# Attention probabilities: weights brought in through a diagonal in the turning product

## The reference, cut to what matters

```
s_s = s_s - slopes[None, :, :, None, None, None] * d_s[:, :, None].astype(f32)
p_s = _masked_softmax(s_s, m_s)
o_s = jnp.einsum('bgrqm,bgqmd->bqgrd', p_s, v_sel)
...
p_w = _masked_softmax(s_w, m_w)
o_w = jnp.einsum('bgrqk,bkgd->bqgrd', p_w, vwb)

return (gb[:, :, 0, :, :, None] * o_c + gb[:, :, 1, :, :, None] * o_s
        + gb[:, :, 2, :, :, None] * o_w)
```

## Time and profile before

| | |
|---|---|
| three runs, median | 1534.01 us (1532.36 to 1534.39) |
| profiled execution | 1536.8 us, span 1535.0 us |
| PE busy | 1368.0 us, 89% of the span |
| DVE busy | 814.4 us, 53% |
| ACT busy | 438.7 us, 29% |
| POOL busy | 908.5 us, 59% |
| mean granted clock of TensorE | 0.956 |
| attention over tokens (first scores to the next stage's first product) | 1003.8 to 1183.4 us |

### The profile page before, as it was taken

One profiled execution on the slowest core, in us unless ns is written; L12 is line 12 of the kernel. 1 busy time (PEld: TensorE's weight loads), 2 busy tenths in 40 slices (PEclk: granted clock), 3 DMA queues, 4 the chain that ended last, 5 costly groups with the idle time before them and its releaser, 6 DMA issues.

```text
span 1535.0 us, 23038 instructions
## 1 busy us (share of the span) xinstructions
PE 1368.0 (89%) x8212; PEld 1059.6 (69%) x8212; DVE 814.4 (53%) x1386; ACT 438.7 (29%) x816; POOL 908.5 (59%) x704
## 2 busy tenths in 40 slices
PE   4979768797999899998959999988898979999986
PEld 2758668684887678887827878745555858878874
DVE  3754797414999921176032904368875136842312
ACT  3025620304321113300051112277765041331102
POOL 3859401073999988899627982900000837658962
PEclk9989978999999999999979999999999989999999
DMA  4213100023332443335717330300001519733321
GB/s 149 69 55 90 55 1 3 7 76 80 97 95 76 171 135 106 96 105 150 232 36 212 96 96 21 97 1 1 2 1 41 206 56 213 221 117 94 97 77 62
DMA packets 86048, 137.95 MB, mean 90 GB/s; under 512 B 16464, under 2 KB 34384, under 8 KB 84816
## 3 DMA queue, kind: packets, MB, share of 16 engines
q1 hardware_dynamic: 48384, 88.10, 19.5%
q10 hardware_dynamic: 37584, 48.71, 10.0%
HBM read 119.02 MB, written 20.91 MB: 91 GB/s over the span
## 4 chain that ended last, share of the span: by engine, by line
PE 74%; DVE 11%; issue 5%; POOL 5%; ACT 4%; DMA 1%; DVEq 0%; ACTq 0%; POOLq 0%
PE ps L353 18%; PE ps L355 18%; PE ps L354 18%; POOL wh L1178 4%; PE ps L346 3%; PE ps L661 3%; PE ps L673 2%; PE ps L650 2%; DVE xs L1245 2%; DVE uL L1235 1%; PE ps L494 1%; PE ps L731 1%; DVE bigB L1675 1%; PE ps L599 1%; DVE bigB L1355 1%
## 5 line engine op out<-in xcount | busy, mean ns | idle before, releaser
L1178 POOL TENSOR_TENSOR wh<-raw,small 128x512 fp32r<-128x512 f32 x336 | 413.4, 1230 | 347.6 <-PE ps L355 336.9
L1180 POOL TENSOR_TENSOR wl<-raw,wh 128x512 fp32r<-128x512 f32 x336 | 482.1, 1435 | 26.3
L353 PE MATMUL ps<-uH,wh 128*128 128x512 f32 x800 | 323.2, 404 | 33.8 <-DVE uL L1235 33.6
L354 PE MATMUL ps<-uL,wh 128*128 128x512 f32 x800 | 317.7, 397 | 0.0
L355 PE MATMUL ps<-uH,wl 128*128 128x512 f32 x800 | 317.3, 397 | 0.0
L353 PEld LDWEIGHTS ps<-uH,wh 128*128 128x128 f32 x800 | 153.7, 192 | 80.1 <-issue 27.7
L355 PEld LDWEIGHTS ps<-uH,wl 128*128 128x128 f32 x800 | 154.0, 193 | 33.0
L354 PEld LDWEIGHTS ps<-uL,wh 128*128 128x128 f32 x800 | 154.2, 193 | 31.0 <-issue 0.5
L353 PE MATMUL ps<-ffH,wh 128*128 128x512 f32 x256 | 102.7, 401 | 17.0 <-POOL wl L1180 16.8
L354 PE MATMUL ps<-ffL,wh 128*128 128x512 f32 x256 | 99.9, 390 | 0.0
L355 PE MATMUL ps<-ffH,wl 128*128 128x512 f32 x256 | 99.8, 390 | 0.0
(11 more groups left out here) (346 smaller groups left out, 2284.5 us busy)
## 6 DMA issues: line engine op xcount, KB each, us to landing
raw<-wstream SPq DMA_DIRECT2D x336, 256.0 KB, 2.6
b_powers_scratch<-bigB ACTq DMA_DIRECT2D x4, 1024.0 KB, 4.8
c_powers_scratch<-bigB ACTq DMA_DIRECT2D x8, 512.0 KB, 4.8
lags_scratch<-lag_rows_scratch ACTq DMA_DIRECT2D x8, 512.0 KB, 7.6
bigB<-b_powers_scratch ACTq DMA_DIRECT2D x4, 1024.0 KB, 8.2
bigB<-lags_scratch ACTq DMA_DIRECT2D x4, 1024.0 KB, 6.7
bigB<-c_powers_scratch ACTq DMA_DIRECT2D x4, 1024.0 KB, 9.5
hT<-x ACTq DMA_DIRECT2D x1, 2048.0 KB, 8.9
```

Source lines behind the costliest of these rows:

```text
L353: pe.matmul(out, lh, rh, start=first, stop=False)
L354: pe.matmul(out, lh, rl, start=False, stop=False)
L1178: pool.tensor_tensor(wh[:, j, :], raw[:, j, :], zero_ap.to_broadcast([128, 512]), ALU.add).then_inc(half_lead, 1)
L1180: pool.tensor_tensor(wl[:, j, :], raw[:, j, :], wh[:, j, :].bitcast(f32), ALU.subtract).then_inc(half_split, 1)
```

## The change

`turn` is no longer a transposing product with the unit matrix but an ordinary product, whose moving operand is a diagonal matrix with the rows' weights. `weigh` no longer touches the probabilities: it multiplies the unit matrix with the weights, for each of the two heads, into a new buffer `diag` (two buffers by u, two heads). It waits until the turn of unit u-2 has read the buffer of the same number.

```
+        diag = place("diag", [128, 2, 2, 128])
...
             def turn(u):
...
                 for half in range(2):
                     for kt in range(qt + 1):
-                        i = pe.transpose(ps[:, 4 + half, kt * 128:(kt + 1) * 128], prob[:, u % 3, half, kt * 128:(kt + 1) * 128], ident)
+                        i = pe.matmul(ps[:, 4 + half, kt * 128:(kt + 1) * 128], prob[:, u % 3, half, kt * 128:(kt + 1) * 128],
+                                      diag[:, u % 2, half, :], start=True, stop=True)
                 i.then_inc(at_t, 1)
...
             def weigh(u):
                 t, qt, b = UNITS[u]
-                W = (qt + 1) * 128
                 dve.wait_ge(at_e, u + 1)
                 own(dve.reciprocal(asum[:, u % 3, :], asum[:, u % 3, :]))
                 own(dve.tensor_tensor(asum[:, u % 3, :], asum[:, u % 3, :], gate[:, qt, 1 + b, t::KT], ALU.mult))
+                if u >= 2:
+                    dve.wait_ge(at_t, u - 1)
                 for half in range(2):
-                    i = dve.tensor_scalar(prob[:, u % 3, half, 0:W], prob[:, u % 3, half, 0:W], asum[:, u % 3, half:half + 1], None, ALU.mult)
+                    i = dve.tensor_scalar(diag[:, u % 2, half, :], ident, asum[:, u % 3, half:half + 1], None, ALU.mult)
                 i.then_inc(at_p, 1)
```

## The result

The changed kernel takes 1554.91 us (median of 4 runs, 1553.65 to 1558.17), the kernel before 1534.2 us in the same series (4 runs). The ratio is 1.014, with a 95% interval of 1.0121 to 1.0159: 20.7 us slower. The profiled execution of the changed kernel is the slowest of its runs, 1558.17 us with a span of 1556.4 us.

The account below looks back on a forecast made before the run. TensorE was taken as nearest to full in the attention stage, busy 18.7 of 21.2 us per head pair. Added passes +35.8, waits -15.3 and clock -3.9 made +16.6 us on 1534.01: forecast 1550.5 us, range 1543 to 1561.

Parts of the forecast that it names:

- the main term: TensorE in the attention stage: 320 turning products cost 0.112 us more each, +35.8 us.
- The second record: Each ordinary turning product leaves two TensorE records instead of one, 640 in all; +35.8 us.
- The gates: TensorE's three waits per head pair, before turns at 1059.43, 1065.95 and 1075.80: 1.96 of 2.51 us gained, 15.3 in all.
- late gates: TensorE's waits before turns of eight products; 1.60 us at 1065.95, with 0.35 taken as left.
- The clock: Two attention periods partly at half clock recover as the long wait mostly goes; -3.9 us.
- Rival 1: Attention stage: clock does not come back, or falls elsewhere; +20.5 us, 1554.5 us; chance 0.25.
- Rival 2: Attention waits stay because VectorE's chain follows a late TensorE; +35.8 less 0 to 5, 1565 to 1570 us; chance 0.08.
- rival 3: The turning product is carried out in one record, so nothing is added on TensorE; 1523 us; chance 0.04.
- rival 4: Loads of weights do not overlap between short turning groups; +88 us on TensorE, 1598 us; chance 0.02.
- The costs of nothing: In attention, VectorE's new wait for unit u-2's turn, the diagonals' buffer and ScalarE's work each add 0.

Follow-up runs that it names:

- e7: Kernel before, with two more 128 x 512 VectorE operations in one unit of each head pair, ahead of its late multiplication; 1545.25 us (one run).
- e8: Changed kernel, with four more 128 x 512 VectorE operations in one unit of each head pair, ahead of the late gate; 1591.08 us (one run).
- e3: Changed kernel without VectorE's new wait for the turn of unit u-2; 1554.94 us, ratio 1.0141.
- e5: Kernel before, but VectorE signals after each head's multiplication and TensorE waits for each head's before turning it; 1523.33 us, ratio 0.9933.
- e9: Kernel of e5, with GpSimd making the slopes only after VectorE's late multiplication of the same unit; 1518.03 us, ratio 0.9899.
- e4: Changed kernel with exponentials and diagonals written in fp32r, so the turning product is an ordinary fp32r one; 1564.39 us, ratio 1.0205.
- e2: Changed kernel's diagonals and new wait, but turning by transposing product with the unit matrix, weights missing from the output; 1518.8 us, ratio 0.9909 against the kernel before.
- e6: Kernel of e4 with each fp32r turning product issued twice to the same place; 1564.9 us (one run).

## Why the prediction was right

Forecast 1550.5 in 1543 to 1561, slower; measured 1554.9. The working held; the main term was too small by 4 us, and the clock's by 0.8.

- **The second record.** 640 records, 0.112 us apart: (1.98 - 0.64) / 12 = 0.112, just line 486's row. But I counted 0.112 us a product and nothing for the group. By the starts, two, four, six and eight products went from 0.36, 0.58, 0.80 and 1.02 us to 0.64, 1.09, 1.54 and 1.98 (before: rows 4 and the two lines of it above, where four products take 0.59 and in other head pairs 0.58; after: above). The differences, 0.28 + 0.51 + 0.74 + 0.96, twice in a period and eight times, are 39.8 us where the term had 35.8. The 4 us are 0.06 us for each of the 64 groups, and make the period 24.15 us where 23.7 to 23.9 were foretold. This is the term that was mis-sized most.
- **The gates.** 15.2 us gained, against 15.3. In a head pair: the first gone as said, the second 0.47 where I took 0.35 (range 0.12 to 0.53), the third gone where 0.2 was left. GpSimd disturbs the short form as well: 0.90 against 0.48 us for a pair (rows above), and without GpSimd the wait is gone. That the sums agree so closely is partly luck. I took all 19.7 us as waits at three gates in eight equal periods; 1.33 of them stand before the stage's first turn and stayed (1.32), and the last two late gates had only 0.86 and 1.28 us to lose. At the gates 3.2 us are left where I left 4.4.
- **The clock.** Behind the filling no stretch of the changed kernel's trace is at half clock. They cost more than the 3.9 us of the sum: the second, from 1131.21 to 1154.81, ends at a late gate where GpSimd does nothing and the wait is 0.86 and not 1.60 us (the line below, of the kernel before). At the full clock it would have been 21.23 - 0.74 = 20.49 us long, so it lost 3.1 us and not 2.37, and both together 4.7. The reason that I gave, the long wait, is supported by e7 and e8 (a longer wait, more half clock), though four of six equal waits before had none. The rule of the Trainium skill that I had left beside it ("TensorE: Matmul & The Clock Gate", Part 4) is not.

```profile
1154.81 1.09 PE L661 MATMUL ps<-const_table,bigB 128*128 128x128 f32 x8 [0.86 <-DVE bigB L1689]
```

- **The rest.** 39.8 - 15.2 - 4.7 = 19.9 us; the stage shows 19.6. The medians differ by 20.7, since they also hold what other stages do: the profiled execution of the changed kernel reached the stage 1.2 us later (1004.98 against 1003.77) and took 0.6 us longer behind it. The clock's term is read from one execution of each kernel. The mean clock of the kernel before goes from 0.954 to 0.966 over its executions, and the profiled one has 0.956; so that the median execution loses 4.7 us too is not shown.
- **The rivals.** Rival 1 named 1554.5 us, the time that was measured, but by a clock that doesn't come back. In the trace it did come back; the number was met by another way, a larger first term. Rival 2 (waits stay) fell with 4.5 us of waits, rival 3 (one record) with 640 records, rival 4 (loads don't overlap) with a spacing of 0.112 us.
- **The costs of nothing.** The new wait: e3 shows 0.0 us. ScalarE: line 675 lost 0.1 us, as before.

The rule of the Trainium skill, "Perfetto Trace Analysis", section "Transposes", to turn with turning products was right in its direction. The factor of four of the Trainium skill, "TensorE: Matmul & The Clock Gate", section "Terms", is two here: 0.224 us against 0.11 us a product.

## What to carry to other kernels

A product with a diagonal in place of turning saves VectorE a pass and costs TensorE a second record per block in fp32. Where TensorE is the fullest engine, as here (18.7 of 21.2 us), count the waits that it can win back (15.2 of 19.7 us here) against the blocks times 0.12 us before making the change. The waits were cheaper to get in two other ways: a signal for each part of the work (e5), and work of another engine moved out of the late operation (e9).

## What was not expected of the hardware

- An ordinary fp32r product of 128 x 128 has the same spacing as a turning record (eight in 1.11 us), but in e4 it came with a mean clock of 0.71 over 194 us (in the slowest execution; over the whole span the other five have 0.930 to 0.936, e2 0.962 to 0.966), and e2, with the same schedule of turning products, with 1.00. In e6 a stretch of 19 us with TensorE busy throughout ran at 0.50.
- Waits of 2.56 to 2.65 us were followed by some 4 us of half clock, or none, with turning products (e7), and by some 7 us with ordinary ones (e8). The cause is open.
- The kernel before itself varied from 1527.24 to 1539.75 us within one series, and its mean granted clock between 0.966 and 0.954. A difference of 4 us between single executions of this kernel says nothing.
